# Even mixer of a hybrid decoder step: convolution taps in two chains, sample taps on GpSimd, transposes and layer norm inside the last projection

## The chip, the cores and the metric

One core of one Trainium2 chip runs the whole program: one inference step of a two-layer decoder trunk. The metric is the device time of one execution in microseconds (us). TensorE (PE), VectorE (DVE), ScalarE (ACT) and GpSimd (POOL) each run their own instruction list in order and wait for one another on counting semaphores. SyncE (SP) issues most DMAs.

## The reference, cut to what matters

512 prompt tokens and 64 sample tokens (8 sequences of 8) share all weights. The change concerns the token mixer of layer 0, the "even mixer":

```
def even_mixer(hn, state, W, j):
    a_val, a_gate, q, k, v, o, gates = jnp.split(hn @ W['ev_w_in'][j], SPLIT_EVEN, axis=-1)
    u = a_val * jax.nn.sigmoid(a_gate)
    full = jnp.concatenate([conv_buf, u], axis=1)
    c = lax.conv_general_dilated(full, taps, ...)          # depthwise, 31 taps, 512 channels
    c = c + W['ev_conv_b'][j]
    mu = jnp.mean(c, axis=-1, keepdims=True)
    var = jnp.mean(jnp.square(c - mu), axis=-1, keepdims=True)
    cn = (c - mu) * lax.rsqrt(var + 1e-5) * W['ev_ln_g'][j] + W['ev_ln_b'][j]
    a_out = jax.nn.silu(cn)
    ...
    h, C1, n1, m1 = mlstm_scan(qh, kh, vh, li, lf, C0, n0, m0)
    b_out = jax.nn.sigmoid(o) * h.reshape(B, T, D_B)
    mix = jnp.concatenate([a_out, b_out], axis=-1) @ W['ev_w_out'][j]
```

Around it stand feed-forward blocks, a second mixer and gated embeddings, which the change does not touch.

## The kernel before

Activations lie as features x tokens: 128 partitions by T = 576 columns (SEQ = 512 of the prompt, then 64 of the samples). A projection is a list of weight blocks of 2048 columns, two output tiles to a block. `gemm` multiplies each tile as 8 steps of three products (rounded weight times rounded input, rounded weight times the input's rest, weight's rest times rounded input), each in two pieces of columns. Output tiles alternate between two places in PSUM (`unit`), so tile t starts only when DVE has read tile t-2 (`normed`, semaphore `tile_evacuated`).

A weight block comes by DMA to `raw`, ACT rounds it to `wr` (`round_block`), and GpSimd forms the rest `wl = raw - wr` (line 515). All three work one block ahead of PE.

The even mixer has three projections of four blocks, eight tiles each: `glu` (value and gate of the convolution), `kv`, and `qo` (q, then o). Between `glu` and `kv` PE forms the gate rows of the mLSTM. DVE then computes on four partitions a chain of row operations (lines 1674 to 1707, here "the row chain"), which comes before the first reading of a `kv` tile on DVE.

The convolution runs on DVE. `conv_chunk(slot)` does about eight of the 31 taps of one 128-channel group j: slots 4j to 4j+3. A tap is a multiply-add over 512 prompt columns into PSUM bank 6 (line 1625) and one over the 64 sample columns into bank 7 (line 1628), alternately, so that a multiply-add never waits for the one just ahead of it. The 16 slots stand between readings of projection tiles: slots 0 to 2 in `glu`, 3 to 8 in `kv`, 9 to 15 in `qo`.

After `kv`, PE turns the last two of its tiles, turns the gate rows into columns, and spreads the samples' rows over partitions, each waiting for a copy by ACT. Then comes `qo`. After `qo` come the layer norm of the convolution (sums over channels as products with `ones`, centering, squares, root, scale, SiLU), the spreading of two mLSTM rows for each of four heads (`spread`, line 678), and the first score products. Then the mLSTM runs head by head (`weigh`, `values`, `states`), and last the output projection.

Of the kernel before, what the change touches and what calls it, by code (L numbers as in the profile page):

```python
# [92 lines left out]
def schedule():  # L93
# [32 lines left out]
def build(nc, A):  # L126
# [91 lines left out]
    wgl = sb("wgl", [P, KD, 36], F32R, at=z)  # L218
    kwm = sb("kwm", [SMP, NB, P], at=z)
    smp = sb("smp", [P, HEADS, 3, SMP], at=z)  # L220
# [285 lines left out]
    def _(e):  # L506
        for s in range(2):
            e.nop().then_inc(S(f"w_split{s}"), 1)
        for name in order:
            p = ph[name]  # L510
            with e.Fori(0, p.nb // 2) as i:  # L511
                for s in range(2):

                    e.wait_ge(S("w_rounded"), i * 2 + (p.n0 + s + 1))
                    e.tensor_tensor(wl[s][:, 0:p.width], raw[s][:, 0:p.width],  # L515
                                    wr[s][:, 0:p.width].bitcast(F32), ALU.subtract
                                    ).then_inc(S(f"w_split{s}"), 1)
# [3 lines left out]
    def _(e):  # L521
# [131 lines left out]
        turn_kv(6)  # L653
        turn_kv(7)

        e.wait_ge(S("rows_exp"), 3)
        e.wait_ge(S("turned_copied"), 16)
        for q, row in enumerate((rowa, rowws)):
            for i in range(ST):
                w = P if i < ST - 1 else SMP  # L660
                o = (q * ST + i) * HEADS
                mm = e.transpose(ps[0:w, 4, o:o + HEADS], row[:, i * P:i * P + w],
                                 C("ident", 0, 4, rows=4))
        mm.then_inc(S("cols_turned"), 1)

        e.wait_ge(S("cols_copied"), 4)
        sel = lambda hh: C("sel", hh * P, (hh + 1) * P, rows=4)
        for hh in range(HEADS):
            o = hh % 2 * 3 * SMP
            mm = e.matmul(ps[:, 4 + hh // 2, o:o + 3 * SMP], sel(hh), rows3[:, :, SEQ:T], start=True, stop=True)  # L670
        mm.then_inc(S("smp_ready"), 1)
        gemm("qo", xin, no_wait)
# [7 lines left out]


        e.wait_ge(S("smp_copied"), 2)
        for j in range(TM):
            if j == TM - 1:
                e.wait_ge(S("tile_evacuated"), evac_at("qo", 7))
                spread(0)
                spread(1)
            e.wait_ge(S("conv_done"), j + 1)
            for hf in range(2):
                mm = e.matmul(ps[:, 4 + hf, 0:HALF], ones[:], cv[:, j, hf * HALF:(hf + 1) * HALF],  # L690
                              start=j == 0, stop=j == TM - 1)
        mm.then_inc(S("ln_sum"), 1)
        spread(2)
        spread(3)

# [55 lines left out]

        e.wait_ge(S("ln_centered"), TM)
        scores(0)
        scores(1)

        for j in range(TM):
            e.wait_ge(S("ln_sq"), j + 1)
            for hf in range(2):  # L760
                mm = e.matmul(ps[:, 6 + hf, 0:HALF], ones[:], (hd, sq)[j % 2][:, hf * HALF:(hf + 1) * HALF],
                              start=j == 0, stop=j == TM - 1)
            mm.then_inc(S("ln_var"), 1)
# [266 lines left out]
    def _(e):  # L1030
# [169 lines left out]
        copy_kv(6)  # L1200
        copy_kv(7)
        e.wait_ge(S("cols_turned"), 1)
        for q in range(2):
            o = q * ST * HEADS
            e.activation(gcol[:, o:o + 16], ps[:, 4, o:o + 16], ACT.Copy).then_inc(S("cols_copied"), 1)
            e.activation(gcol[0:SMP, o + 16:o + 20], ps[0:SMP, 4, o + 16:o + 20], ACT.Copy
                         ).then_inc(S("cols_copied"), 1)
        e.wait_ge(S("smp_ready"), 1)
        for q in range(2):
            e.activation(smp[:, 2 * q:2 * q + 2], ps[:, 4 + q, 0:6 * SMP].rearrange("p (h q t) -> p h q t", h=2, q=3),  # L1210
                         ACT.Copy).then_inc(S("smp_copied"), 1)
        for n in blocks("qo"):
            if n >= 2:
                for o in (2 * (n - 2), 2 * (n - 2) + 1):
                    e.wait_ge(S("tile_evacuated"), evac_at("qo", 4 + o))
                    e.activation(oT[:, o, :], tu[:], ACT.Sigmoid).then_inc(S("o_ready"), 1)
# [16 lines left out]
        copy_spread(0)  # L1233
        copy_spread(1)

        e.wait_ge(S("conv_stored"), 16 * (1 + TM))
        for j in range(TM):
            e.wait_ge(S("ln_centered"), j + 1)
            if j >= 2:
                e.wait_ge(S("ln_var"), j - 1)  # L1240
            e.activation((hd, sq)[j % 2][:], cv[:, j, :], ACT.Square).then_inc(S("ln_sq"), 1)
            if j % 2:
                decay(j // 2)

        e.wait_ge(S("ln_var"), TM)
        e.activation(two(acc[:]), ps[:, 6:8, 0:HALF], ACT.Ln, scale=1.0 / DA, bias=eps5[:, 0:1]
                     ).then_inc(S("ln_root"), 1)
        e.wait_ge(S("ln_root"), 1)
        e.activation(acc[:], acc[:], ACT.Exp, scale=-0.5).then_inc(S("ln_root"), 1)
        copy_spread(2)  # L1250
        copy_spread(3)
        for j in range(TM):
            e.wait_ge(S("ln_scaled"), j + 1)
            e.activation(cv[:, j, :], cv[:, j, :], ACT.Silu, scale=W("ln_g", j), bias=W("ln_b", j)
                         ).then_inc(S("conv_out"), 1)
            e.wait_ge(S("conv_out"), j + 1)
            e.activation(xr[:, j, :], cv[:, j, :], ACT.Copy).then_inc(S("mixr_ready"), 1)

# [214 lines left out]
    def _(e):  # L1473
# [137 lines left out]
        accp, accs = ps[:, 6, 0:SEQ], ps[:, 7, 0:SMP].rearrange("p (b t) -> p b t", b=NB)  # L1611

        def tap(j, k, outp, outs, sem=None, wait=None):
# [4 lines left out]
            inp = up[:, j, bass.ds(k, SEQ)]  # L1618
            ins_ = us[:, j, :, bass.ds(k, TB)]
            if wait is None:  # L1620
                a = e.tensor_scalar(outp, inp, w, W("conv_b", j), ALU.mult, ALU.add)
                a.then_inc(S("conv_step"), 1)
                b = e.tensor_scalar(outs, ins_, w, W("conv_b", j), ALU.mult, ALU.add)
            else:
                a = e.scalar_tensor_tensor(outp, inp, w, accp, ALU.mult, ALU.add)
                a.then_inc(S("conv_step"), 1)
# [664 lines left out]
```

## Time and profile before

| what | us |
|---|---|
| median of 3 timed runs | 2624.3 (2612.31 to 2625.74) |
| the profiled execution | 2605.91 |
| its span, first to last instruction | 2604.1 |

The granted clock of TensorE was 0.979 of full speed on average. The profiled execution was shorter than each of the timed runs; durations below are all from it. A wait row names who waited and who ended the wait, and a row of a timeline gives the start, the duration, and in brackets the idle time of the engine just before.

### The profile page before, as it was taken

How to read it: one execution, taken by the hardware profiler on the slowest of the kernel's cores; microseconds unless marked ns; L12 is line 12 of the kernel's file. 1: busy time of each engine (PE TensorE's matmuls, PEld its weight loads, DVE VectorE, ACT ScalarE, POOL GpSimd, SP SyncE). 2: the span in 40 equal slices, each digit the busy share in tenths (PEclk: the TensorE clock that was granted, in tenths of full speed). 3: DMA queues.
4: the chain of work that ended last, by engine and by line, in shares of the span. 5: the costliest groups of instructions: out<-in, count | busy, mean ns of one | idle time of the engine just before them, and what ended most of it. 6: DMA issues, size and time to landing. Idle time of an engine off the chain costs nothing.

```text
span 2604.1 us, 44896 instructions
## 1 busy us (share of the span) xinstructions
PE 2501.4 (96%) x18512; PEld 2401.8 (92%) x18512; DVE 852.9 (33%) x1438; ACT 760.3 (29%) x904; POOL 809.2 (31%) x204
## 2 busy tenths in 40 slices
PE   7999999998779999999999999999989999999997
PEld 7999999987469999999999999999955799999997
DVE  3220222678563220223422112221176532202224
ACT  4221224222323221223432222231155532212232
POOL 3334334322003333333333333343200133343332
PEclk9999999998789999999999999999999999999999
DMA  4222223411112222212222222133442122222222
GB/s 149 81 82 90 81 68 108 93 66 49 34 52 90 81 69 92 91 68 81 83 97 89 73 98 85 63 104 118 145 135 82 49 91 81 77 90 78 70 81 77
DMA packets 67047, 220.67 MB, mean 85 GB/s; under 512 B 14022, under 2 KB 31302, under 8 KB 51338
## 3 DMA queue, kind: packets, MB, share of 16 engines
q1 hardware_dynamic: 56112, 202.84, 23.3%
q10 hardware_dynamic: 10842, 16.53, 2.3%
q8 instruction: 66, 1.08, 0.2%
q14 instruction: 27, 0.22, 0.0%
HBM read 208.02 MB, written 11.33 MB: 84 GB/s over the span
## 4 chain that ended last, share of the span: by engine, by line
issue 55%; PE 31%; POOL 11%; DVE 2%; ACT 0%; POOLq 0%; DMA 0%; DVEq 0%
PE ps L556 26%; POOL wl L515 11%; PE ps L939 2%; DVE rows L1962 0%; PE ps L913 0%; PE ps L825 0%; PE ps L969 0%; PE ps L817 0%; DVE tiny L1965 0%; POOLq L511 0%; PE ps L959 0%; PE ps L587 0%; DVE h L2133 0%; DVE stick L2045 0%; PE ps L991 0%
## 5 line engine op out<-in xcount | busy, mean ns | idle before, releaser
L515 POOL TENSOR_TENSOR wl<-raw,wr 128x2048 fp32r<-128x2048 f32 (+2 forms) x200 | 809.0, 4045 | 1769.6 <-ACT wr L1048 1769.6
L556 PE MATMUL ps<-xr,wr 128*128 128x256 f32 (+1 forms) x2304 | 500.0, 299 | 24.1 <-POOL wl L515 20.0
L556 PE MATMUL ps<-xl,wr 128*128 128x256 f32 (+1 forms) x2304 | 496.6, 297 | 0.0
L556 PE MATMUL ps<-xr,wl 128*128 128x256 f32 (+1 forms) x2304 | 496.0, 297 | 0.0
L1048 ACT ACTIVATE wr<-raw 128x2048 fp32r<-128x2048 f32 (+1 forms) x200 | 351.6, 1758 | 372.0 <-PE ps L556 298.8
L556 PEld LDWEIGHTS ps<-xr,wr 128*128 128x128 f32 x2304 | 390.5, 191 | 27.1 <-issue 19.9
L556 PEld LDWEIGHTS ps<-xl,wr 128*128 128x128 f32 x2304 | 391.1, 191 | 0.0
L556 PEld LDWEIGHTS ps<-xr,wl 128*128 128x128 f32 x2304 | 390.6, 191 | 0.0
L556 PE MATMUL ps<-x2r,wr 128*128 128x256 f32 (+1 forms) x1664 | 354.5, 294 | 0.9 <-POOL wl L515 0.9
L556 PE MATMUL ps<-x2l,wr 128*128 128x256 f32 (+1 forms) x1664 | 353.6, 293 | 0.0
L556 PE MATMUL ps<-x2r,wl 128*128 128x256 f32 (+1 forms) x1664 | 353.5, 293 | 0.0
L556 PE MATMUL ps<-hr,wr 128*128 128x256 f32 x1472 | 313.0, 294 | 0.0
L556 PE MATMUL ps<-hl,wr 128*128 128x256 f32 x1472 | 312.9, 293 | 0.0
L556 PE MATMUL ps<-hr,wl 128*128 128x256 f32 x1472 | 312.8, 293 | 0.0
L556 PEld LDWEIGHTS ps<-x2r,wr 128*128 128x128 f32 x1664 | 277.3, 187 | 1.9 <-issue 1.5
L556 PEld LDWEIGHTS ps<-x2r,wl 128*128 128x128 f32 x1664 | 277.3, 187 | 0.0
L556 PEld LDWEIGHTS ps<-x2l,wr 128*128 128x128 f32 x1664 | 277.1, 187 | 0.0
L556 PEld LDWEIGHTS ps<-hr,wr 128*128 128x128 f32 x1472 | 245.1, 187 | 1.3 <-DVE tu L1521 0.9
L556 PEld LDWEIGHTS ps<-hl,wr 128*128 128x128 f32 x1472 | 245.2, 188 | 0.0
L556 PEld LDWEIGHTS ps<-hr,wl 128*128 128x128 f32 x1472 | 245.2, 187 | 0.0
L1521 DVE TENSOR_TENSOR tu<-ps,R 128x576 f32<-128x576 f32 x96 | 72.7, 758 | 499.9 <-PE ps L556 499.9
L1102 ACT ACTIVATE hr<-hd 128x576 f32 (+1 forms) x88 | 60.5, 687 | 577.9 <-DVE hd L1537 577.9
(305 smaller groups left out, 1852.4 us busy)
## 6 DMA issues: line engine op xcount, KB each, us to landing
raw<-in_up SPq DMA_DIRECT2D x88, 1024.0 KB, 4.9
raw<-in_down SPq DMA_DIRECT2D x32, 768.0 KB, 4.2
raw<-in_mixin SPq DMA_DIRECT2D x24, 1024.0 KB, 4.9
raw<-in_down SPq DMA_DIRECT2D x32, 640.0 KB, 3.9
raw<-in_ple SPq DMA_DIRECT2D x16, 640.0 KB, 3.9
raw<-in_mixout SPq DMA_DIRECT2D x8, 1024.0 KB, 4.9
kc<-in_kc SPq DMA_DIRECT2D x32, 256.0 KB, 3.5
vc<-in_vc SPq DMA_DIRECT2D x32, 256.0 KB, 3.0
```

Source lines behind the costliest of these rows:

```text
L515: e.tensor_tensor(wl[s][:, 0:p.width], raw[s][:, 0:p.width], wr[s][:, 0:p.width].bitcast(F32), ALU.subtract).then_inc(S(f"w_split{s}"), 1)
L556: mm = e.matmul(piece(u, hf), w_[:, a:b], x_[:, x0:x1], start=n_k == 0 and n_ == 0, stop=n_k == kn_ - 1 and n_ == 2)
L939: mm = e.matmul(ps[:, 2 + c, o:w], C("after" if j == i else "later"), stick[hh % 2][:, c, at:at + w - o], start=j == i, stop=j == TM - 1)
L1048: e.activation(wr[slot][:, 0:w], raw[slot][:, 0:w], ACT.Copy).then_inc(S("w_rounded"), 1)
L1102: e.activation(column(hr, i * 2 + s), hd[:], ACT.Copy).then_inc(S("hr_ready"), 1)
L1521: ins = e.tensor_tensor(out, unit(u), R[:], ALU.mult)
```

## The change

- The last projection is renamed `oq` and makes o's four tiles first, then q's; the host's order of weight tiles follows.
- The prompt's taps go in two chains: even steps add up in PSUM bank 6, odd ones in bank 7. A tap waits for the tap before the last. A final addition joins the two.
- The samples' taps go to GpSimd (`conv_of_samples`): for half of a channel group, one product over 32 positions x 31 taps, four halving additions, one last addition and the bias, each waiting for the one before. Eight such halves stand behind the splits of blocks `glu` 2 to `oq` 1.
- The slots move forward: 0 to 6 in `glu`, 7 to 13 in `kv`, 14 and 15 in `oq`.
- PE's work between `kv` and the last projection, and the two products of the layer norm, stand between tiles of `oq`. ACT's copies, squares, root and SiLU, and DVE's centering and scaling, move with them.
- The rounding of the convolution's output (`xr`), the input of the output projection, stays behind `oq`.

```
+        def conv_of_samples(n):
+            j, half = divmod(n, 2)
+            e.wait_ge(S("u_ready"), 2 * j + 2)
...
+            e.tensor_tensor(prods[:].rearrange("p (b t) k -> p b t k", t=TB), windows,
+                            taps.unsqueeze(1).unsqueeze(1).broadcast_to([P, NB // 2, TB, TAPS]), ALU.mult
+                            ).then_inc(S("sample_added"), 1)
+            for a, b in ((15, 16), (8, 8), (4, 4), (2, 2)):
+                e.wait_ge(S("sample_added"), added[0])
+                e.tensor_tensor(prods[:, :, 0:a], prods[:, :, 0:a], prods[:, :, b:b + a], ALU.add
+                                ).then_inc(S("sample_added"), 1)
...
+        SAMPLES_BEHIND = {("glu", 2): 0, ("glu", 3): 1, ("kv", 0): 2, ("kv", 1): 3, ("kv", 2): 4, ("kv", 3): 5,
+                          ("oq", 0): 6, ("oq", 1): 7}
...
-        turn_kv(6)
-        turn_kv(7)
...
+        beside_oq = {0: lambda: turn_kv(6), 1: lambda: turn_kv(7), 2: turn_gates, 3: spread_samples, 5: ln_sums,
+                     6: ln_squares}
+        gemm("oq", xin, no_wait, lambda t: beside_oq[t]() if t in beside_oq else None)
...
+        e.wait_ge(S("tile_evacuated"), evac_at("oq", 7))
         e.wait_ge(S("ln_centered"), TM)
+        spread(0)
         scores(0)
+        spread(1)
         scores(1)
+        spread(2)
+        spread(3)
...
-            if wait is not None:
-                e.wait_ge(S("conv_step"), wait - 1)
...
-                b = e.scalar_tensor_tensor(outs, ins_, w, accs, ALU.mult, ALU.add)
+            e.wait_ge(S("conv_step"), n - 1)
+            e.scalar_tensor_tensor(chain[q], up[:, j, bass.ds(k, SEQ)], w, chain[q], ALU.mult, ALU.add
+                                   ).then_inc(S("conv_step"), 1)
...
-            if j < TM - 1:
-                conv_chunk(j)
+            for slot in ((0,), (1, 2), (3, 4), (5, 6))[j]:
+                conv_chunk(slot)
...
-            if t >= 2:
-                conv_chunk(t + 1)
+            if t:
+                conv_chunk(6 + t)
...
+            if t < 2:
+                conv_chunk(14 + t)
+            if t == 5:
+                e.wait_ge(S("ln_sum"), 1)
+                for j in range(TM):
+                    e.scalar_tensor_tensor(two(cv[:, j, :]), psn, -1.0 / DA, two(cv[:, j, :]), ALU.mult, ALU.add
+                                           ).then_inc(S("ln_centered"), 1)
+            if t == 6:
+                e.wait_ge(S("ln_root"), 2)
+                for j in range(TM):
+                    e.tensor_tensor(cv[:, j, :], cv[:, j, :], acc[:], ALU.mult).then_inc(S("ln_scaled"), 1)
```

The order of instructions at three places follows. First DVE at the end of `glu`: the readings of tiles 6 and 7 (`tg`, `tu`), the convolution's input `up` and `us`, and the start of the row chain (`rowa`). Before:

```order
L1521 TENSOR_TENSOR tg<-ps,R 128x576 [waits tile_done]
L1521 TENSOR_TENSOR tu<-ps,R 128x576 [waits tile_done]
L1660 TENSOR_TENSOR up<-tg,sg 128x512 [waits tile_evacuated,glu_sig]
L1661 TENSOR_TENSOR us<-tg,sg 128x8x8
L1674 TENSOR_TENSOR rowa<-ps,R 4x576 [waits gates_done,u_ready]
L1675 TENSOR_TENSOR rowt<-ps,R 4x576
```

After the change (one of the two loops of taps, slot 6, shown; each loop body has two taps):

```order
L1702 UNCONDITIONAL_BRANCH
L1702 ISA
L1685 ISA [waits conv_step]
L1685 SCALAR_TENSOR_TENSOR ps<-up,prm,ps 128x512
L1684 REGISTER_ALU
L1685 ISA [waits conv_step]
L1685 SCALAR_TENSOR_TENSOR ps<-up,prm,ps 128x512
L1702 REGISTER_ALU
L1702 COMPARE_AND_BRANCH
L1734 TENSOR_TENSOR rowa<-ps,R 4x576 [waits gates_done]
L1735 TENSOR_TENSOR rowt<-ps,R 4x576
```

The row chain stood right behind `us`; now sixteen taps stand between them, and the sample instruction (L1628) is gone from the loop.

Second, GpSimd behind the split of a block in the changed kernel, where before one split followed the other:

```order
L515 TENSOR_TENSOR wl_55<-raw_52,wr_54 128x2048 [waits w_rounded]
L531 TENSOR_TENSOR prods<-us,prm 128x992 [waits sample_conv,u_ready]
L537 TENSOR_TENSOR prods<-prods 128x32x15 [waits sample_added]
L537 TENSOR_TENSOR prods<-prods 128x32x8 [waits sample_added]
L537 TENSOR_TENSOR prods<-prods 128x32x4 [waits sample_added]
L537 TENSOR_TENSOR prods<-prods 128x32x2 [waits sample_added]
L542 TENSOR_TENSOR cv<-prods 128x32 [waits sample_added]
L545 TENSOR_SCALAR cv<-cv,prm 128x32 [waits sample_added]
L515 TENSOR_TENSOR wl_57<-raw_53,wr_56 128x2048 [waits w_rounded]
```

Seven short instructions came between two splits.

Third, PE behind the last tile of the last projection. Before (the sums of the layer norm's last group, spreading, scores, the first of the squares):

```order
L690 MATMUL ps<-cv,ones 128x288 [waits conv_done]
L690 MATMUL ps<-cv,ones 128x288
L678 MATMUL ps<-rows_100,cst 128x512 [waits bcast_copied]
L678 MATMUL ps<-rows_100,cst 128x512
L678 MATMUL ps<-rows_100,cst 128x512 [waits bcast_copied]
L678 MATMUL ps<-rows_100,cst 128x512
L707 MATMUL ps<-qT,kT 128x512 [waits ln_centered]
L707 MATMUL ps<-qT,kT 128x384
L761 MATMUL ps<-hd,ones 128x288 [waits ln_sq]
```

After:

```order
L746 MATMUL ps<-rows_100,cst 128x512 [waits ln_centered,tile_evacuated]
L746 MATMUL ps<-rows_100,cst 128x512
L757 MATMUL ps<-qT,kT 128x512
L746 MATMUL ps<-rows_100,cst 128x512 x2
L757 MATMUL ps<-qT,kT 128x384
L746 MATMUL ps<-rows_100,cst 128x512 [waits bcast_copied]
L746 MATMUL ps<-rows_100,cst 128x512
L746 MATMUL ps<-rows_100,cst 128x512 [waits bcast_copied]
L746 MATMUL ps<-rows_100,cst 128x512
L770 MATMUL ps<-tg,vn 128x512 [waits p_ready,vn_ones,bcast_copied]
```

The products with `ones` have left this place, and the first value product (L770) follows the spreading directly.

## Rows read from the trace of the kernel before

**Rows 1.** The page: busy time of each engine over the span.

```profile
PE 2501.4 (96%) x18512; PEld 2401.8 (92%) x18512; DVE 852.9 (33%) x1438; ACT 760.3 (29%) x904; POOL 809.2 (31%) x204
```

**Rows 2.** Busy time by stretch; PEclk is the granted clock of TensorE.

```profile
core 0: us, PE busy (x) PEld busy (x) DVE busy (x) ACT busy (x) POOL busy (x), PEclk, DMA share, GB/s
505.00:561.10 56.10, 54.58 (x415) 54.34 (x414) 46.97 (x92) 15.82 (x21) 18.77 (x4) 1.00 0.46 81
561.10:572.20 11.10, 5.67 (x31) 4.45 (x28) 10.91 (x24) 2.62 (x10) 0.00 (x0) 0.77 0.01 2
572.20:577.30 5.10, 5.10 (x22) 5.09 (x22) 1.46 (x4) 2.67 (x3) 2.24 (x1) 0.50 0.00 2
577.30:637.80 60.50, 52.10 (x378) 50.65 (x376) 55.43 (x116) 9.02 (x8) 16.30 (x4) 0.98 0.20 70
637.80:654.20 16.40, 16.40 (x20) 6.12 (x20) 3.48 (x6) 5.99 (x9) 0.00 (x0) 0.50 0.00 0
654.20:674.10 19.90, 13.90 (x33) 7.58 (x32) 7.94 (x14) 12.96 (x19) 0.00 (x0) 0.79 0.03 4
```

**Rows 3.** Timeline of DVE in `glu`: tile readings, taps.

```profile
473.23 0.76 DVE L1521 TENSOR_TENSOR tu<-ps,R 128x576 f32<-128x576 f32 x1 [1.32 <-PE ps L556]
...
476.01 0.76 DVE L1625 SCALAR_TENSOR_TENSOR ps<-up,prm,ps 128x512 f32<-128x512 f32 x1 [0.44 <-DVE us L1661]
476.67 0.28 DVE L1628 SCALAR_TENSOR_TENSOR ps<-us,prm,ps 128x64 f32<-128x64 f32 x1
476.94 0.76 DVE L1625 SCALAR_TENSOR_TENSOR ps<-up,prm,ps 128x512 f32<-128x512 f32 x1
...
483.63 0.75 DVE L1521 TENSOR_TENSOR tg<-ps,R 128x576 f32<-128x576 f32 x1
486.03 0.76 DVE L1521 TENSOR_TENSOR tu<-ps,R 128x576 f32<-128x576 f32 x1 [1.64 <-PE ps L556]
```

**Rows 4.** Timeline of DVE: the row chain and the first readings of `kv`.

```profile
505.22 0.75 DVE L1674 TENSOR_TENSOR rowa<-ps,R 4x576 f32<-4x576 f32 x1 [4.06 <-PE ps L527]
...
510.67 2.15 DVE L1689 SCALAR_TENSOR_TENSOR rowt<-rowt,rowB 4x576 f32<-4x576 f32 x1 [1.59 <-ACT rowB L1188]
...
518.28 0.20 DVE L1707 TENSOR_TENSOR rowws<-rowa,rows 4x64 f32<-4x64 f32 x1
518.51 1.42 DVE L1523 SCALAR_TENSOR_TENSOR kT<-ps,R 128x576 f32<-128x576 f32 x2
```

**Rows 5.** Timeline of POOL: the split beside that row chain.

```profile
507.29 4.92 POOL L515 TENSOR_TENSOR wl<-raw,wr 128x2048 fp32r<-128x2048 f32 x1 [13.28 <-ACT wr L1048]
```

**Rows 6.** Groups of DVE, 300 to 900 us: an addition's kind with two SBUF inputs.

```profile
L1537 DVE TENSOR_TENSOR hd<-tu,sg 128x576 f32<-128x576 f32 x13 | 9.8, 758 | 0.5
```

**Rows 7.** Groups of POOL by shape, whole span: busy us, mean ns.

```profile
L515 POOL TENSOR_TENSOR wl<-raw,wr 128x2048 fp32r<-128x2048 f32 x120 | 554.9, 4624 | 1294.4 <-ACT wr L1048 1294.4
L515 POOL TENSOR_TENSOR wl<-raw,wr 128x1280 fp32r<-128x1280 f32 x48 | 141.8, 2955 | 272.2 <-ACT wr L1048 272.2
```

**Rows 8.** Timeline of PE: turning, sample rows, spreading, scores, sums of squares.

```profile
560.62 0.71 PE L645 MATMUL ps<-cst,sq 128*128 128x128 f32 x5
...
569.35 2.92 PE L670 MATMUL ps<-rows,cst 4*128 4x192 f32 x8 [0.45 <-ACT gcol L1206]
...
637.76 7.19 PE L678 MATMUL ps<-rows,cst 4*128 4x512 f32 x8 [5.90 <-DVE tu L1521]
...
654.22 3.35 PE L707 MATMUL ps<-qT,kT 128*128 128x512 f32 x4
...
659.27 1.13 PE L761 MATMUL ps<-sq,ones 128*128 128x288 f32 x4
```

**Rows 9.** Timeline of ACT, then of DVE: rounding of the convolution's output, and the next gap of `weigh`.

```profile
671.08 0.68 ACT L1257 ACTIVATE xr<-cv 128x576 fp32r<-128x576 f32 x1
...
674.06 0.29 DVE L1734 TENSOR_SCALAR Xs<-Mb,gcol 128x128 f32<-128x128 f32 x1
```

More of the change, by code:

```diff
@@ L509, in _ @@
+        SAMPLES_BEHIND = {("glu", 2): 0, ("glu", 3): 1, ("kv", 0): 2, ("kv", 1): 3, ("kv", 2): 4, ("kv", 3): 5,
+                          ("oq", 0): 6, ("oq", 1): 7}
         for name in order:
             p = ph[name]
+            if name in ("glu", "kv", "oq"):
+                for n in range(p.nb):
+                    split(p, n // 2, n % 2)
+                    if (name, n) in SAMPLES_BEHIND:
+                        conv_of_samples(SAMPLES_BEHIND[name, n])
+                continue
             with e.Fori(0, p.nb // 2) as i:
@@ L664, in _, with turn_gates @@
-        mm.then_inc(S("cols_turned"), 1)
-        e.wait_ge(S("cols_copied"), 4)
-        sel = lambda hh: C("sel", hh * P, (hh + 1) * P, rows=4)
[L668 to L672, printed above, removed]
+        def turn_gates():
+            e.wait_ge(S("rows_exp"), 3)
+            e.wait_ge(S("turned_copied"), 16)
+            for q, row in enumerate((rowa, rowws)):
+                for i in range(ST):
+                    w = P if i < ST - 1 else SMP
+                    o = (q * ST + i) * HEADS
+                    mm = e.transpose(ps[0:w, 4, o:o + HEADS], row[:, i * P:i * P + w],
+                                     C("ident", 0, 4, rows=4))
+            mm.then_inc(S("cols_turned"), 1)
@@ new lines, in ln_squares @@
+        def ln_squares():
+            for j in range(TM):
+                e.wait_ge(S("ln_sq"), j + 1)
+                for hf in range(2):
+                    mm = e.matmul(ps[:, 6 + hf, 0:HALF], ones[:], (hd, sq)[j % 2][:, hf * HALF:(hf + 1) * HALF],
+                                  start=j == 0, stop=j == TM - 1)
+                mm.then_inc(S("ln_var"), 1)
+        beside_oq = {0: lambda: turn_kv(6), 1: lambda: turn_kv(7), 2: turn_gates, 3: spread_samples, 5: ln_sums,
+                     6: ln_squares}
@@ L679, in spread @@
             mm.then_inc(S("bcast_ready"), 1)
[L682 to L694, printed above, removed]
         def scores(k):
@@ L1212, in _, with copy_gates @@
[L1212 to L1216, printed above, removed]
+        def copy_gates():
+            e.wait_ge(S("cols_turned"), 1)
+            for q in range(2):
+                o = q * ST * HEADS
+                e.activation(gcol[:, o:o + 16], ps[:, 4, o:o + 16], ACT.Copy).then_inc(S("cols_copied"), 1)
+                e.activation(gcol[0:SMP, o + 16:o + 20], ps[0:SMP, 4, o + 16:o + 20], ACT.Copy
+                             ).then_inc(S("cols_copied"), 1)
@@ L1233, in _ @@
         copy_spread(0)
+        decay(0)
         copy_spread(1)
-        e.wait_ge(S("conv_stored"), 16 * (1 + TM))
+        decay(1)
+        for hh in (2, 3):
+            copy_spread(hh)
         for j in range(TM):
[L1238 to L1255, printed above, removed]
+            e.wait_ge(S("tile_done"), done_at("oq", 7))
             e.wait_ge(S("conv_out"), j + 1)
             e.activation(xr[:, j, :], cv[:, j, :], ACT.Copy).then_inc(S("mixr_ready"), 1)
+        e.wait_ge(S("conv_stored"), 16 * (1 + TM))
+        e.wait_ge(S("conv_done"), TM)
+        e.wait_ge(S("sample_conv"), 2 * TM)
         def load_state(hh):
@@ L1752, in weigh @@
             e.tensor_tensor(pm[0:r, 0:n], pm[0:r, 0:n], m, ALU.mult).then_inc(S("p_ready"), 1)
-        e.wait_ge(S("ln_sum"), 1)
-        for j in range(TM):
-            e.scalar_tensor_tensor(two(cv[:, j, :]), psn, -1.0 / DA, two(cv[:, j, :]), ALU.mult, ALU.add
-                                   ).then_inc(S("ln_centered"), 1)
         e.wait_ge(S("bcast_copied"), 2)
@@ L1764, in _ @@
         weigh(1)
-        e.wait_ge(S("ln_root"), 2)
-        for j in range(TM):
-            e.tensor_tensor(cv[:, j, :], cv[:, j, :], acc[:], ALU.mult).then_inc(S("ln_scaled"), 1)
         for j in range(TM):
```

158 lines of the change are left out of this document (97 added, 61 removed).

## The prediction

> **What bounds the kernel now.** I read the page first: PE is busy for 96% of the span, DVE for a third [rows 1]. So outside the even mixer another engine's work is free, and a gain must come from stretches in which PE stands idle or runs cold. The table by stretch shows four such places. Over `kv` (505.0 to 561.1 us) PE is nearly full at full clock. In the 11.1 us behind it PE is half busy, with turning and spreading that wait for ACT's copies. The 5.1 us after that run at a granted clock of 0.50. The last projection then takes until 637.8, though DVE is busy for 55.4 of its last 60.5 us: DVE sets the pace there, not PE. From 637.8 to 674.1 PE does layer norm and spreading, at first at clock 0.50 [rows 2].
>
> The timeline of DVE gives the prices. Two tiles of a projection are 12.8 us apart on PE (473.23 and 486.03, the readings of the odd tiles, each just after its tile ends), so a tile is 6.4 us. A prompt tap has 0.66 us from its start to the next instruction's, though it lasts 0.76; a pair of prompt and sample takes 0.93 to 1.0 [rows 3]. Eight pairs (about 7.7 us) and a reading are longer than 6.4, which is why DVE leads in the last projection.
>
> **The change part by part.** The sum compares times on the profiled execution, up to the start of `weigh`'s fourth gap, at 674.06 [rows 9]; what follows is the same in both.
>
> *Taps in `glu`.* Without the sample instruction a tap should cost 0.66, the pair's 0.97 less some 0.3. This trace has no two taps in a row; the bounds are 0.66 and 0.76, a tap's whole duration, if the next must wait for its end. I take 0.66, since it is the row's distance to an instruction that depends on the tap before the last, as now. But the slots move forward. Behind group 1's input come two slots instead of one: 476.01 + 16 x 0.66 + 0.2 for two loop entries = 486.8, then the reading of tile 4, to 487.5. PE wanted its place at 485.8: it waits 1.7. Tile 5 is read at once; from such a reading to the next first tap there are 2.78 us (473.23 to 476.01), so slots 3 and 4 start at 490.2. They hold 12 taps (7.9), two opening products (1.4), the last tap and its dependent addition (1.5) and entries (0.2): until 501.3. Two readings and again 2.78 lead to 504.7; slots 5 and 6 last 10.8, until 515.5.
>
> *The row chain* stood right behind; it began at 505.22 and the first reading of `kv` at 518.51 [rows 4], 13.3 us. It now begins at 515.5 and ends at 528.8. This is the wait that the change adds: behind the chain on DVE stands the reading of `kv` tiles 0 and 1, and PE's tile 2 waits for that. PE has done tiles 0 and 1 at about 519.6 and then has nothing: its third tile starts some 10.3 us later than before.
>
> *The chain beside GpSimd.* In the chain one multiply-add of 4x576 with two SBUF inputs took 2.15 us [rows 4] where a larger two-input operation takes 0.76 [rows 6]; a split on GpSimd ran from 507.29 to 512.21 [rows 5], and the slow one ended 0.6 after that. So a two-input instruction stood still until GpSimd's ended. The tap, with one input in PSUM, keeps 0.76 beside a split. Now GpSimd works through most of the chain's time, first a half of samples, then a split. Five long operations of the chain have two SBUF inputs. Between none of them hit (-1.4) and one behind a whole split (4.6), one behind a product (2.3) and some behind short additions (1), I take +2, little over what was seen once. PE's tile 2 of `kv`: 10.3 + 2 = **+12.3**.
>
> The Trainium skill (SBUF — State Buffer, § SBUF: two separate sides) says that DVE's two-input operations and GpSimd share a port pair as an exclusive lock, held for the whole instruction by whoever starts first. By that rule the delay is the upper end, about +8, and the forecast falls by 6; the slow row of the chain agrees with it, but how often the two meet depends on instants.
>
> *The clock after that wait.* Behind the idle stretch at 561 to 572 the clock was 0.50 for 5.1 us of the next projection [rows 2]: half of that, 2.5 us, was lost. An idle time of some 12 us in `kv` should cost the same: **+2.5** (bounds 0 and 5). From there `kv` runs at PE's pace: a tile and a turning are under 7 us, a reading and a slot 0.7 + 5.5.
>
> *Behind `kv`.* Its 11.1 us go: **-11.1**.
>
> *The last projection.* Before: 572.2 to 637.8, 65.6 us. After: eight tiles, 51.2; two turnings at 0.5 (five products took 0.71 to the end of the last), the gate columns 1, the sample rows 1.5 (2.92 at half clock), two rounds of four sums at 1.13 each, 9.0 [rows 8]; then the reading of the last tile, 0.9. With 1 us for the hand-overs of the squares and 0.5 for DVE's scaling, a two-input operation beside the split of the next block, this makes 66.1: **+0.5**. DVE no longer leads: two slots are left here, and centering and scaling (four operations each of 0.67) fit beside a tile.
>
> *Behind it.* Before: 637.8 to 674.06, 36.3 us. What is left: the spreading of four heads, twice the row of 7.19, and the scores, 3.35, all at clock 0.50 [rows 2, 8], so 17.7, or 8.9 at full clock; the copy of the last pair, 1.2, four roundings, 0.6 from start to start (0.68 each, [rows 9]), and the last subtraction, 0.8. That is 13.2 at full clock and 22.0 at half. PE comes warm from the projection; but 16.4 us of such work at 100% busy did not lift the clock before [rows 2], so it may fall on the way. I take full clock for all but some 2 us: 15.3, so **-21** (bounds -14.3 and -23.1).
>
> *Samples on GpSimd.* Two shapes give 2.17 ns a column and 0.175 us for an instruction [rows 7]. A half has 992 + 480 + 256 + 128 + 64 + 32 + 32 = 1984 columns in seven instructions: 4.3 + 1.2 + waits of some 0.5, about 6.0 us. With its split, 4.6, that is 10.6 of a block's 12.8. The next split is wanted 12.8 us after this one, and PE wants its result 6 us after that. So I put it at nothing; its cover ends at 8.2 us a half, and much of what it overruns is hidden by the wait in `kv`.
>
> Sum: 12.3 + 2.5 - 11.1 + 0.5 - 21 = -16.8, say **-17**: a span of 2587 where it was 2604.1. The execution lasted 2605.91, that is 18.4 below the median of the timed runs, 2624.3; I apply the difference to the median: **2607 us**. A change under 0.5%, 13 us, can't be told from none; the runs before lie 13 us apart.
>
> **The rivals.**
>
> *The port decides (0.12).* The chain's two-input operations wait +8 instead of +2, and the scaling another 2. The row of 2.15 speaks for it; against it, DVE also takes turns, and five operations can't all fall on long ones. 17 - 8 = 9 gained: 2615, no change.
>
> *Spreading runs cold (0.08).* -14.3 instead of -21: 10 gained, 2614. For it: the clock row of 637.8 to 654.2; against: that stretch began after 6 us without PE work.
>
> *The chains buy little (0.07).* If a tap takes 0.97 as the pair did, 44 taps up to the row chain add 0.31 x 44 = 13.6 to the wait in `kv`, and a slot of 7.8 with its reading paces `kv` again: 2621 to 2626, no change. At 0.76 it is 0.1 x 44 = 4.4, and 2611.
>
> *GpSimd is the bound (0.12), slower.* From its first split with a half, 463.8, GpSimd has eight splits and halves and then the split for the third block of the last projection, which PE wants at about 605. With c for a half, that split ends at 463.8 + 8 x (4.6 + c) + 4.6. The gain of 17 is gone when this is 622, at c = 14.6, 2.4 times my estimate or 1.2 us more per instruction. At 18 us it ends at 649: 44 late, a loss of 27, 2651. For it: no row shows a short, strided or broadcast instruction there, or a scalar operation; against: 0.175 us is all that the two shapes leave for the start of one.
>
> **How the numbers follow.** The forecast's own case, a gain of 13 to 24 (2600 to 2611), has 0.54; a gain beyond that, with none of the port's waits and everything warm, 0.07. Faster is 0.61. Same: 0.12 + 0.08 + 0.07 = 0.27. Slower: 0.12. With the bounds of the terms (port -1.4 to +8, clock 0 to 5, spreading -14.3 to -23.1) the gain runs from 2 to 25; with the timed runs' spread of 13 around the median the range is 2589 to 2627, which leaves out most of the slower case and the extremes.
>
> **What the changed profile would show.** Right: taps of one group 0.66 apart; PE idle in `kv` before tile 2 for 10 to 14 us, ended by DVE's reading, with clock 0.50 behind it; no idle stretch between `kv` and the last projection; that projection in about 65 us with 9 us of products with `ones` in it; the fourth gap of `weigh` near 657. It would be wrong if PE waits for splits (line 515), if halves of samples last over 8 us, or if that idle in `kv` is much under 8 or over 18 us.

## The result, and the profile after

Timed, the changed kernel takes 2603.2 us (median of 7 runs, 2596.4 to 2608.0), the kernel before 2613.6 (7 runs, 2609.3 to 2625.7): a ratio of 0.9931, with a 95% interval of 0.9911 to 0.995. The profiled execution took 2601.26 us for a span of 2599.5; before, the span was 2604.1. The medians differ by 10 us, the ratio says 18, the two spans 4.6. The runs of the kernel before lie in two groups, at 2609 to 2614 and at 2624 to 2626 us, so its median and each ratio to it depend on how many runs fall in the upper one; with the longer times the record shows a lower mean granted clock (2609 us at 0.977, 2626 at 0.971, in runs timed beside the experiments), and no trace of a longer run was taken. And behind the changed part, where the programs are the same, the two profiled executions are 4 us apart (1930.0 us from the fourth gap to the end before, 1934.0 after). So the parts of the change are read at points inside it, up to the fourth gap of `weigh`, as the prediction did.

The same points after, first the page's busy time, to be held against [rows 1], then the busy time by stretch, against [rows 2] (PEclk is the granted clock of TensorE):

```profile
PE 2497.4 (96%) x18512; PEld 2401.3 (92%) x18512; DVE 834.3 (32%) x1318; ACT 759.7 (29%) x904; POOL 856.0 (33%) x260
```

```profile
core 0: us, PE busy (x) PEld busy (x) DVE busy (x) ACT busy (x) POOL busy (x), PEclk, DMA share, GB/s
519.00:535.40 16.40, 0.15 (x2) 0.04 (x1) 15.28 (x15) 4.52 (x6) 13.79 (x12) 0.58 0.30 108
535.40:538.60 3.20, 3.20 (x13) 3.20 (x14) 3.20 (x6) 0.00 (x0) 0.00 (x0) 0.50 0.00 0
538.60:578.50 39.90, 39.90 (x306) 39.90 (x305) 33.04 (x50) 7.37 (x12) 20.43 (x16) 1.00 0.15 54
578.50:643.60 65.10, 63.02 (x448) 60.23 (x445) 31.05 (x41) 23.66 (x33) 24.02 (x11) 1.00 0.18 59
643.60:644.50 0.90, 0.82 (x2) 0.48 (x3) 0.03 (x1) 0.88 (x2) 0.00 (x0) 1.00 0.93 391
644.50:664.90 20.40, 19.23 (x23) 6.19 (x22) 5.12 (x11) 8.90 (x16) 0.00 (x0) 0.50 0.13 42
```

The reader is to see three things. PE now stands idle for 16.2 us in `kv`, ahead of its tile 2, and for the 3.2 us behind that it runs at clock 0.50. From 538.6 to 643.6 there is no idle stretch between `kv` and the last projection, which takes 65.1 us. And from 644.5 on, with PE busy nearly all the time, the clock is 0.50 for 20.4 us.

What PE waited for, from `glu` to the start of the spreading (us in total, times, longest):

```profile
PE ps L598 <- DVE kT L1591: 16.2, 1, 16.2
PE ps L746 <- DVE qT L1589: 2.2, 1, 2.2
PE ps L598 <- DVE tg L1589: 1.4, 1, 1.4
```

The row chain on DVE, which stands before that reading of `kT`; it answers to [rows 4] (start, duration, operation):

```profile
514.14 0.74 DVE L1734 TENSOR_TENSOR rowa<-ps,R 4x576 f32<-4x576 f32 x1
...
515.69 1.10 DVE L1737 TENSOR_SCALAR rowa<-rowa,prm 4x576 f32<-4x576 f32 x1
516.72 1.48 DVE L1738 TENSOR_SCALAR rowt<-rowt,prm 4x576 f32<-4x576 f32 x1
...
522.54 4.87 DVE L1753 TENSOR_TENSOR rowa<-rowa,rowB 4x576 f32<-4x576 f32 x1
527.44 2.29 DVE L1756 COPY rowt<-rowa 4x576 f32<-4x576 f32 x1
529.76 1.07 DVE L1759 TENSOR_TENSOR rowt<-rowa,prm 4x8 f32<-4x8 f32 x1
...
534.49 1.42 DVE L1591 SCALAR_TENSOR_TENSOR kT<-ps,R 128x576 f32<-128x576 f32 x2
```

And GpSimd (POOL) beside it: a split, a half of samples (product, additions), the next split, the next half:

```profile
514.27 2.21 POOL L531 TENSOR_TENSOR prods<-us,prm 128x992 f32<-128x992 f32 x1
516.55 3.24 POOL L537 TENSOR_TENSOR prods<-prods 128x480 f32<-128x480 f32 x4
...
522.23 4.57 POOL L515 TENSOR_TENSOR wl<-raw,wr 128x2048 fp32r<-128x2048 f32 x1 [1.64 <-ACT wr L1096]
526.76 2.66 POOL L531 TENSOR_TENSOR prods<-us,prm 128x992 f32<-128x992 f32 x1
529.50 4.88 POOL L537 TENSOR_TENSOR prods<-prods 128x480 f32<-128x480 f32 x4
```

The chain lasts 20.3 us where it took 13.3. Put the two lists side by side: the subtraction of 4.87 us starts 0.3 us behind the start of the split at 522.23 and ends 0.6 behind its end; the copy of 2.29 us starts within the product of 526.76 and ends 0.3 behind its end; an operation on 4x8 numbers takes 1.07 us.

Behind the last projection (PE, then DVE; it answers to [rows 8, 9]):

```profile
643.68 2.87 PE L746 MATMUL ps<-rows,cst 4*128 4x512 f32 x4 [2.17 <-DVE qT L1589]
646.48 2.08 PE L757 MATMUL ps<-qT,kT 128*128 128x512 f32 x2
648.48 3.78 PE L746 MATMUL ps<-rows,cst 4*128 4x512 f32 x4
...
653.77 7.19 PE L746 MATMUL ps<-rows,cst 4*128 4x512 f32 x8
```

```profile
665.49 0.29 DVE L1804 TENSOR_SCALAR Xs<-Mb,gcol 128x128 f32<-128x128 f32 x1
```

The fourth gap of `weigh` stands at 665.49, where it was at 674.06: 8.6 us earlier. The last eight of the 16 spreading products take as long as before, 7.19 us.

### The profile page after: what moved, and what is told of

Read it like the earlier page. It is cut to its first block, busy times and chain, and to the rows that moved or that the text cites. A ratio compares the mean times of both kernels' runs of the same rounds, so it can differ in the third digit from the quotient of the medians.

```text
span 2599.5 us, 44514 instructions
## 1 busy us (share of the span) xinstructions
PE 2497.4 (96%) x18512; PEld 2401.3 (92%) x18512; DVE 834.3 (32%) x1318; ACT 759.7 (29%) x904; POOL 856.0 (33%) x260
## 4 chain that ended last, share of the span: by engine, by line
PE 50%; issue 37%; POOL 7%; DVE 3%; ACT 1%; DVEq 0%; POOLq 0%; DMA 0%
PE ps L598 46%; POOL wl L515 7%; PE ps L987 2%; DVE ps L1685 0%; DVE rows L2024 0%; PE ps L873 0%; PE ps L961 0%; PE ps L1017 0%; PE ps L629 0%; PE ps L687 0%; PE ps L865 0%; DVE tiny L2027 0%; PE ps L1007 0%; DVE h L2195 0%; PE ps L645 0%
```

## The experiments

Nine kernels were timed, in three sets on three chips, each set with the kernel before beside it; that had medians of 2622.9 (the late slots, the halves, the taps, the full height), 2613.7 (the split, the 32 rows, the five products, the four edits) and 2616.3 (the order). The ratios are those to the kernel before in the same set. Two numbers compare the kernels with the changed kernel: the place of the fourth gap in the trace, and the median.

| kernel | median | ratio to the kernel before (95% interval) | fourth gap | against the changed kernel: gap, median |
|---|---|---|---|---|
| before | 2613.6 | 1 | 674.06 | +8.6, +10.4 |
| changed | 2603.2 | 0.9931 (0.9911 to 0.995) | 665.49 | |
| late slots | 2589.2 | 0.9884 (0.9858 to 0.9909) | 652.92 | -12.6, -14.0 |
| halves off the chain | 2598.0 | 0.9911 (0.989 to 0.9931) | 663.50 | -2.0, -5.2 |
| taps only | 2611.5 | 0.9953 (0.9934 to 0.9972) | 672.07 | +6.6, +8.3 |
| order only | 2615.6 | 0.9991 (0.9977 to 1.0005) | 680.51 | +15.0, +12.4 |
| split after scaling | 2603.4 | 0.9961 (0.9948 to 0.9974) | 663.57 | -1.9, +0.1 |
| full height | 2594.9 | 0.9895 (0.9873 to 0.9916) | 659.12 | -6.4, -8.3 |
| 32 rows | 2602.2 | 0.9954 (0.9932 to 0.9975) | 666.43 | +0.9, -1.0 |
| five products | 2628.6 | 1.0061 (1.004 to 1.0082) | 690.68 | +25.2, +25.4 |
| four edits | 2577.2 | 0.9866 (0.9848 to 0.9884) | 640.71 | -24.8, -26.0 |

The last column's two numbers agree within 3.2 us for every kernel, across the sets. The ratios of different sets agree less well, because the kernel before moves under them. A gap also carries what the execution was early or late ahead of the changed work: at the reading of `glu`'s second tile (460.06 us in the changed kernel) the halves stand 1.6 us later, the order 1.4, the four edits 1.3 and the others up to 0.7. Without that the halves gain 3.6 on the changed kernel and the four edits 26.0, the order loses 13.6, and the change itself gained 8.2.

**The slots later.** The row chain starts later because slots were put ahead of it.

```
-            for slot in ((0,), (1, 2), (3, 4), (5, 6))[j]:
+            for slot in ((0,), (1,), (2,), ())[j]:
...
-            if t:
-                conv_chunk(6 + t)
+            conv_chunk(3 + t)
...
-            if t < 2:
-                conv_chunk(14 + t)
+            if t < 5:
+                conv_chunk(11 + t)
```

> Edit: behind the gated inputs of glu stand slots 0, 1 and 2 alone, one for each of the first three groups; 3 to 10 follow the eight readings of kv, 11 to 15 the first five of the last projection. My account (the idle time of 16.25 us in kv is the row chain's late start, 514.1, and the rest of its 20.3 us is the port): the chain starts at 503 to 504, lasts between 13.3 and 20.3 us and ends at 517 to 524; PE wants the place of kv's tile 2 at about 519, so that wait falls to 0 to 5 us, the stretch at granted clock 0.50 behind it goes, and the kernel gains 12 to 17 on the changed one: 2586 to 2592. Rival 1: the five slots that now lie in the last projection make DVE its pace-maker again (before, DVE was busy for 55.4 of 60.5 us there): that projection takes 70 us or more instead of 65, and the kernel gains under 8: 2595 or more. Rival 2: the length of the chain is what GpSimd makes of it wherever it stands, and it meets a split and two halves here too, lasting 25 us or more: 2595 or more, with a wait of 10 us left in kv.

2589.2 us; the fourth gap comes 12.6 earlier. The wait for `kT` is 5.0 us, and the last projection has no new wait. My account held, but for two points: the chain started at 505.10, not at 503 to 504, and the cold stretch behind the wait did not go, the clock was 0.50 from 522.7 to 525.8. The chain ended at 521.87: its rows on DVE show that GpSimd beside it still costs 3.5 us, and that a scan, which has two inputs in SBUF too, is held up as well (it takes 1.35 alone):

```profile
510.68 2.04 DVE L1749 SCALAR_TENSOR_TENSOR rowt<-rowt,rowB 4x576 f32<-4x576 f32 x1 [1.72 <-ACT rowB L1236]
512.76 3.25 DVE L1751 TENSOR_TENSOR_SCAN rowB<-rows,rowt 4x576 f32<-4x576 f32 x1
516.04 1.61 DVE L1753 TENSOR_TENSOR rowa<-rowa,rowB 4x576 f32<-4x576 f32 x1
```

**The halves away from the chain.**

```
-        SAMPLES_BEHIND = {("glu", 2): 0, ("glu", 3): 1, ("kv", 0): 2, ("kv", 1): 3, ("kv", 2): 4, ("kv", 3): 5,
-                          ("oq", 0): 6, ("oq", 1): 7}
+        SAMPLES_BEHIND = {("glu", 2): (0,), ("glu", 3): (1,), ("kv", 0): (2, 3), ("kv", 3): (4,),
+                          ("oq", 0): (5,), ("oq", 1): (6,), ("oq", 2): (7,)}
...
```

> Edit: the two halves of samples that GpSimd works on while the row chain runs (514 to 521 and 527 to 535) are put elsewhere, one behind kv's first split beside the half that is there, the others a block later each; the splits stay. My account (DVE's operations of the chain stood behind GpSimd's instructions): the scalar additions (1.10 and 1.48 us) go back to some 0.5, the copy (2.29) to 0.45, the maximum (1.07) to 0.16, the last addition (1.15) to 0.75; only the subtraction (4.87) behind the split stays. The chain lasts 15 instead of 20.3 us, the wait for kT falls from 16.25 to about 11, and the kernel comes to about 2598. Rival: what slows the chain is the splits, or operations that wait for each other, and not the halves: the chain stays within 2 us of 20.3 and the time at 2603.

2598.0 us. The chain's rows (DVE), the same operations as in the list above:

```profile
517.43 0.74 DVE L1734 TENSOR_TENSOR rowa<-ps,R 4x576 f32<-4x576 f32 x1
...
518.98 0.51 DVE L1737 TENSOR_SCALAR rowa<-rowa,prm 4x576 f32<-4x576 f32 x1
519.42 0.50 DVE L1738 TENSOR_SCALAR rowt<-rowt,prm 4x576 f32<-4x576 f32 x1
...
524.26 4.87 DVE L1753 TENSOR_TENSOR rowa<-rowa,rowB 4x576 f32<-4x576 f32 x1
529.16 0.45 DVE L1756 COPY rowt<-rowa 4x576 f32<-4x576 f32 x1
529.64 0.16 DVE L1759 TENSOR_TENSOR rowt<-rowa,prm 4x8 f32<-4x8 f32 x1
...
532.66 1.42 DVE L1591 SCALAR_TENSOR_TENSOR kT<-ps,R 128x576 f32<-128x576 f32 x2
```

Each went to the duration expected of it, and the subtraction behind the split alone stayed. The chain takes 15.2 us, so GpSimd's instructions are shown to be what slows it. The time gained less than the 5 us of the chain: the half that was moved forward met DVE's two-input multiplications of `glu` instead (1.37 and 1.26 us where they take 0.69 and 0.22). That put the start of the chain 1.7 us later; the other 1.6 of its 3.3 (to 517.43) this execution was late already in `glu`. The wait for `kT` fell to 12.9, not 11, and the gain is 2.0 by the fourth gap, 3.6 without the late start, and 5 by the medians, where I expected 5.

**One half of the change at a time.** First the taps in two chains and the samples on GpSimd, everything else, the slots too, as before:

> Edit: the kernel before, with q before o, the turning and the layer norm behind the projection and its slots at their old places, but with the taps in two chains and the samples' taps on GpSimd. My account (before, DVE led in the last projection, 65.6 us where PE needs 51.2 and a reading): the projection takes 52 to 54 us, the row chain loses 0 to 7 us beside GpSimd, the cold stretches stay. A gain of 6 to 13 on the kernel before, so by its median of 2613.6 of the runs here 2600 to 2607: as much as the whole change gave. Rival: what the change gave came from the new order on PE, and the cheaper taps alone move work off an engine that ended no wait: within 4 us of the kernel before.

2611.5 us, 0.9953: 11 us under the kernel before in its set, as expected, but that stood at 2622.9 there. By its own median, where I expected 2600 to 2607, and by the fourth gap, 2.0 earlier than before, it is hardly faster. The projection does what I expected: its tiles, read up to 8.3 us apart before, come every 6.40 (592.04, 598.44, 604.84, 611.24). But the row chain takes 24.4 us beside the halves, 11 more than before and well over my 0 to 7, and gives that back. Here an operation with one input in SBUF stood behind a whole split, and one on 4x64 numbers too:

```profile
507.43 4.88 DVE L1713 TENSOR_SCALAR rowt<-rowt,prm 4x576 f32<-4x576 f32 x1
...
521.85 4.50 DVE L1739 TENSOR_TENSOR rows<-prm,rows 4x64 f32<-4x64 f32 x1
```

Then the other half, the new order on PE and ACT with o before q and the slots as in the changed kernel, but with the old taps:

> Edit: the other half of the undoing. The new order on PE and ACT, o before q and the slots at the changed kernel's places stay; the taps are the old ones again, pairs of a prompt's and a sample's instruction on DVE, and GpSimd has its splits alone. My account (the new order needs the cheap taps): the pairs of 0.97 instead of 0.66 us put the row chain some 10 to 14 us later, to 524 to 528; without halves beside it, it lasts 13 to 18 us; so kv's tile 2 waits 22 to 28 us instead of 16, and a slot with its reading, 8.5 us, paces the tiles of kv behind it (7 tiles, 1.6 us each over PE's 6.95): 2613 to 2627, no gain on the kernel before or a loss. Rival: the order on PE is what gave the gain, and DVE's longer slots hide beside PE's turning and layer norm: within 5 us of the changed kernel, 2599 to 2608.

2615.6 us, 0.9991: no gain, and by the fourth gap 6.5 later than before. The chain started at 529.61, and PE waited 18.4 us for `kT` (I expected 22 to 28) and 6.3 instead of 1.4 for a tile of `glu`. DVE read the tiles of `kv` behind that mostly 8.28 us apart, but PE still turned one every 6.95 (574.44, 581.39, 588.34) and paid only at the end of `kv`, with 2.6 and 1.1 us of waiting for ACT's copies of the last tiles. Without halves on GpSimd the chain takes 15.2 us. So neither half is worth much alone: at the fourth gap the taps bring 2.0, the order costs 6.5, and both together bring 8.6. With the old taps the new order starts the row chain 15 us later still, and with the halves of samples beside it the chain of the old order is 11 us longer.

**The split behind the scaling.** In the changed kernel the first scaling on DVE takes 3.93 us beside GpSimd's split for the output projection.

```
+            if name == ("out", 0):
+                e.wait_ge(S("ln_scaled"), TM)
```

> Edit: GpSimd's split for the first block of the output projection waits until DVE has scaled all four groups. My account: DVE's first scaling (3.93 us in the changed kernel, beside that split) takes 0.75, so the reading of the last tile comes about 2.2 to 3.2 us earlier and PE's wait of 2.2 us ahead of the spreading goes. On the clock that leaves two theories. A: the clock falls behind the idle time of 2.5 us ahead of the spreading; without it the spreading starts and stays at 1.00, and the kernel gains 8 to 12: 2591 to 2595. B: the products with four rows do not hold the clock; it falls all the same some microseconds into them, and the gain is the 2 us alone: 2600 to 2602.

2603.4 us. The four scalings take 2.77 us instead of 5.94 together, PE's wait ahead of the spreading is 0.8 instead of 2.2, the fourth gap comes 1.9 earlier, and the clock falls all the same, 2.1 us into the spreading (theory B). The medians show nothing of the 1.9 (theory B gave 2600 to 2602). The clock:

```profile
642.70:644.90 2.20, 2.09 (x5) 0.84 (x6) 0.06 (x1) 0.57 (x2) 2.20 (x1) 1.00 0.00 0
644.90:663.50 18.60, 17.42 (x20) 5.83 (x21) 5.65 (x11) 7.90 (x15) 0.10 (x1) 0.50 0.33 109
```

**The spreading at full height.** The products that spread rows over the partitions take four rows of the array.

```
-    rows3 = sb("rows3", [HEADS, 3, T], at=z)
+    rows_all = sb("rows_all", [P, 3, T], at=z)
+    rows3 = rows_all[0:HEADS]
...
-            for q, row in enumerate((rowM, rowem)):
-                mm = e.matmul(ps[:, 2 * (hh % 2) + q, :], sel(hh), row[:, 0:SEQ], start=True, stop=True)
+            for q in range(2):
+                mm = e.matmul(ps[:, 2 * (hh % 2) + q, :], C("sel", hh * P, (hh + 1) * P), rows_all[:, q, 0:SEQ],
+                              start=True, stop=True)
...
+        step(e.memset(rows_all[:, 0:2, 0:SEQ], 0.0))
+        settle()
```

> Edit: the rows that are spread over the partitions stand in a block of 128 rows of which 124 are zero, and the products that spread them take all 128 rows instead of four; two memsets ahead of glu (1024 columns each 128 rows) are added; the result is the same. Theory 1 (TensorE ran at granted clock 0.50 from 644.4 to 664.9 because it did products with four rows there): the spreading and the scores run at 1.00, spread products of 0.9 instead of 1.8 us each, and the fourth gap comes 7 to 9 us earlier: 2594 to 2597. Theory 2 (the clock falls for another reason, the wait of 2.2 us ahead of it or the waits for copies within it): the clock stays at 0.50 there and the time within 3 us of 2603.

2594.9 us. The clock by stretch, from the spreading to the fourth gap:

```profile
644.20:645.70 1.50, 1.44 (x3) 0.68 (x4) 0.00 (x1) 1.48 (x2) 0.00 (x0) 0.96 0.61 257
645.70:649.00 3.30, 3.30 (x5) 1.35 (x4) 0.82 (x2) 1.95 (x4) 0.00 (x0) 0.50 0.00 0
649.00:659.10 10.10, 8.92 (x24) 4.21 (x23) 4.86 (x9) 6.33 (x13) 0.00 (x0) 1.00 0.30 103
```

The clock falls here too, but comes back after 3.3 us, and eight spreading products take 3.60 us instead of 7.19:

```profile
651.00 3.60 PE L747 MATMUL ps<-rows_all,cst 128*128 128x512 f32 x8
```

The fourth gap is at 659.12, 14.9 us behind the start of the spreading, where it was 21.8: 6.4 us earlier, a little under the 7 to 9 expected. Theory 1, then, with a correction: the clock falls with 128 rows too, so here the four rows are not shown to make it fall; they keep it down. The same with a block of 32 rows:

> Edit: as the spreading with 128 rows, but the block has 32 rows (28 of them zero). The 128 rows brought the clock back to 1.00 after 3.4 us where four rows left it at 0.50 for 20.5. If what brings it back is how much of the array's height a product fills, 32 rows lie between: I expect that they do not do it, a cold stretch of over 15 us and 2600 to 2605. If anything above four rows does it: a cold stretch of some 3.4 us and 2593 to 2597.

2602.2 us. The clock stayed down, as with four:

```profile
644.20:644.90 0.70, 0.63 (x2) 0.39 (x3) 0.01 (x1) 0.68 (x2) 0.00 (x0) 0.98 1.06 445
644.90:666.40 21.50, 20.32 (x24) 6.67 (x23) 5.67 (x11) 9.09 (x16) 0.00 (x0) 0.50 0.14 50
```

PE was busy for 20.32 of those 21.50 us. Keeping PE busy was not enough, then.

**GpSimd loaded.** To see how near the slower rival was, each half makes its products five times.

```
+            for again in range(5):
+                if again:
+                    e.wait_ge(S("sample_added"), added[0])
...
```

> Edit: in each half GpSimd makes the products of the samples five times in a row instead of once, with the same result. A half then takes 6.1 + 4 x 2.25 = 15.1 us, just over the 14.6 from which the prediction let GpSimd eat the whole gain. By the working of that rival the split for the third block of the last projection ends at 463.4 + 8 x (4.6 + 15.1) + 4.6 = 625.6, and PE wants it at about 607: waits of 18 us in all for splits, and 0 to 5 us more of the row chain beside more products. 2620 to 2626. Against it: GpSimd is idle for long stretches in kv, and the late splits hide in the idle time of 16 us there; then under 8 us are lost, 2603 to 2611.

2628.6 us, slower than the kernel before (1.0061). The first half took 15.4 us. PE's waits:

```profile
PE ps L601 <- DVE kT L1594: 23.3, 1, 23.3
PE ps L601 <- POOL wl L515: 7.2, 2, 4.9
PE ps L601 <- DVE tg L1592: 3.5, 1, 3.5
```

The size was nearly right (2620 to 2626 expected), the way only in part. Waits for splits are 7.2 us and not 18; as much, 7.1, was lost at `kT` and 2.1 more at `tg`, because DVE's gated inputs in `glu` and the row chain stood behind the products; the rest of the 25 us is not split up here. The first of these inputs:

```profile
491.10 2.41 DVE L1724 TENSOR_TENSOR up<-tg,sg 128x512 f32<-128x512 f32 x1 [0.75 <-ACT sg L1212]
```

**The edits together.** The late slots, the split behind the scaling, the spreading at full height, and no half behind the split that runs beside the chain.

> Edit: the late slots, the spreading with 128 rows and the split behind the scaling together, and of the samples' halves none behind the split that runs beside the row chain (the others follow one block later). My account adds the terms: the row chain lasts 13.3 to 14 us from 505, so of the wait of 16.25 us in kv 0 to 1.5 are left and the cold 1.6 behind it go (-16 to -18), the wait of 2.2 ahead of the spreading goes (-2), and the spreading is cold for at most 3.4 us (-6 to -8). Together -24 to -28 on the changed kernel: 2575 to 2579, 0.983 to 0.985 of the kernel before. Rival: the edits get in each other's way, the last half of samples, which now stands behind the third split of the last projection, or the slot in its fifth tile holds up the layer norm's sums: 2585 or more, with a wait for GpSimd or DVE in that projection.

2577.2 us, the fastest of all, 26 under the changed kernel and 0.9866 of the kernel before (I expected 0.983 to 0.985). The clock and PE's waits:

```profile
627.40:640.70 13.30, 11.97 (x30) 5.65 (x31) 5.77 (x12) 8.51 (x16) 2.35 (x1) 1.00 0.44 151
```

```profile
PE ps L601 <- DVE kT L1595: 1.8, 1, 1.8
PE ps L749 <- DVE qT L1593: 0.8, 1, 0.8
```

The row chain takes 13.6 us, the wait for `kT` is 1.8, and the spreading up to the fourth gap (640.71) runs at 1.00 throughout, in 13.3 us. The terms add up as expected, 24.8 us at the fourth gap, but for one: behind the wait of only 1.8 us in `kv` the clock still averaged 0.53 from 521.2 to 524.6, where I had counted that cold stretch as gone.

## Why the prediction came out as it did

The forecast was 2607, a gain of 17 on 2624.3; measured was 2603.2, a gain of 10 on 2613.6, and 8.6 at the fourth gap. The time fits by luck, because two errors met: the median of three runs that I subtracted from, 2624.3, lies 10.7 us above the median of seven; and the gain is half of what I had. Term by term, each between the same two points of both traces:

| from, to | forecast | measured |
|---|---|---|
| start of the row chain | +10.3 | +8.9 (505.22 to 514.14) |
| length of the row chain | +2 | +7.0 (13.3 to 20.3) |
| from the first reading of `kv` to the spreading: clock, tail, last projection | +2.5 - 11.1 + 0.5 = -8.1 | -10.1 (119.3 to 109.2) |
| from the spreading to the fourth gap | -21 | -14.5 (36.3 to 21.8) |
| sum, rounding aside | -17 | -8.6 |

*Taps and slots: right.* Four taps in a row took 2.73 us at 0.75 each, so 0.66 apart; the place in `glu` was waited for 1.4 us (forecast 1.7). The half of samples takes 6.1 us where DVE leaves it alone (forecast 6.0), and no split was waited for. But the half beside the end of the row chain took 8.4 (526.76 to 535.17), over the 8 that I had named as a sign of being wrong: DVE held GpSimd up in turn, which I had not thought of, and the next split, at 553.74, hid it.

*The chain beside GpSimd: the mechanism right, the size not.* I took +2 between -1.4 and +8; it is +7, near the +8 of the rival "the port decides" (0.12). Of the 7, the subtraction behind the whole split is 4.1, a case that stood in my bounds and got little weight; the two scalar additions and the copy are 3.4, which stood nowhere; shorter two-input operations are 1.7; and the multiply-add and a wait for ACT gave back 2.2. So the step that failed is that I counted "five long operations of the chain" with two SBUF inputs, and little on those. The traces show one-input operations between SBUF and SBUF held up as well: the scalar additions, the copy, and, with the taps alone, 4.88 us for one behind a whole split. Away from the halves they take 0.45 to 0.51 for 576 columns, where a two-input operation takes 0.75. The Trainium skill (VectorE: DVE Perf Modes, § Mode 2×_2P) says that such an operation reads one tensor through both ports, which these durations agree with, and (SBUF — State Buffer, § SBUF: two separate sides) that this mode asks for the shared pair too. The section was in front of me, and I used only half of its rule. Taps, with an input in PSUM, were not held up, as forecast.

*The wait in `kv`: right in kind, too small.* 16.2 us, where I gave 10 to 14; the excess comes from the length of the chain, which started 1.4 earlier than forecast. The clock behind it cost less than forecast: 3.2 us at 0.50, some 1.6.

*From `kv` to the spreading: 2 better than forecast.* Half of it is the clock in `kv`, 1.5 us from PE's first product of tile 2 to its sixth turning (42.7 us where it was 41.2) instead of 2.5. The other half is the last projection: 65.1 us is 1.0 under the forecast in spite of 2.2 us of waiting for the scaling, the first of which took 3.93 beside a split, 3.2 more than alone, where I had 0.5. The 11.1 us behind `kv` went as forecast, though not only for the reason that I gave, "turning and spreading that wait for ACT's copies": in the kernel before, DVE read the last tiles of `kv` 8.3 us apart while PE turned one every 6.95, and the longest wait there was for DVE's late reading of `sg` (rows of DVE, then of PE):

```profile
549.83 0.75 DVE L1521 TENSOR_TENSOR sq<-ps,R 128x576 f32<-128x576 f32 x1
558.12 0.75 DVE L1521 TENSOR_TENSOR tg<-ps,R 128x576 f32<-128x576 f32 x1
...
546.73 0.71 PE L645 MATMUL ps<-cst,kT 128*128 128x128 f32 x5
...
553.68 0.71 PE L645 MATMUL ps<-cst,hd 128*128 128x128 f32 x5
...
566.11 0.77 PE L645 MATMUL ps<-cst,sg 128*128 128x128 f32 x5 [3.11 <-DVE sg L1521]
```

*Behind the projection: the step that failed.* "PE comes warm from the projection", and I took full clock for all but 2 us. It came warm, and 0.8 us into the spreading the clock was 0.50, for 20.4 us. What I had put in the rival, 0.08, is what happened: -14.5, between its -14.3 and my -21. My evidence against it, that the cold stretch before "began after 6 us without PE work", did not decide: with only 0.8 us of waiting left the clock fell as well, with 128 rows behind 2.2 us of waiting it recovered, and in the four edits together, with 128 rows behind 0.8 us, it did not fall there at all. At full clock the stretch takes 13.3 us, which is what I had worked out for it (13.2). The Trainium skill (TensorE: Matmul & The Clock Gate, § Part 1) ties the gate to how busy PE has been; here PE at 94% busy stayed at the lower level when most of its products filled 4 or 32 rows, and the measurement decides.

*The slower rival.* At 15.4 us a half the gain was gone and more, but the larger part of the waits that came with it was for DVE, which stood behind GpSimd (9.2 us), and not for late splits (7.2).

The change as a whole: the cheap taps and the new order need each other, as the two halves show. What they could have brought went into the wait for the row chain (16 us) and into a spreading at half clock (8 us). Of these the late slots gave back 12.6, the full height 6.4 (by the fourth gap).

What stays open: why the clock fell in the spreading with 128 rows when that edit stood alone (3.3 us) and not with the other edits. The wait ahead of the spreading was 2.2 us in the one and 0.8 in the other, and no run separates that from the rest.

## What to carry to other kernels

Work that is taken off a waiting engine must not be put ahead of what the bound engine waits for: ask at each place where slots are filled which instruction stands behind them. Before moving work to GpSimd, list all that DVE does meanwhile between SBUF and SBUF, with one input or two, however small, and count the whole length of GpSimd's instruction for what meets it. And before counting on TensorE's full clock, look at how many rows its products fill, not only at whether it is busy: that was worth 6.4 us here.

## What the hardware showed that was not expected

- TensorE's granted clock stayed at 0.50 (1.2 GHz) for 20.4 us in which most products fill 4 rows (19.2 us of it busy) and for 21.5 us with 32 rows; with 128 rows, 124 of them zero, it was back at 1.00 (2.4 GHz) after 3.3 us.
- The cold stretch did not grow with the wait: behind 16.2 us without PE work in `kv` the clock was 0.50 for 3.2 us, behind 12.9 (halves) for 4.9, behind 5.0 (late slots) for 3.1, and behind 1.8 (four edits) it averaged 0.53 for 3.4.
- DVE's one-input fp32 operations from SBUF to SBUF were held up by a running GpSimd instruction: 4.88 us instead of 0.50 behind a split, 2.29 instead of 0.45 for a copy. Memsets beside GpSimd kept their 0.54 us.
- It goes both ways: GpSimd's four additions took 4.88 us beside the chain, 3.24 beside less of it, 3.06 away from it.
- GpSimd's short instructions cost little: 0.26 us for an addition of 32 columns and 0.36 for a scalar one, where the straight line through two long shapes left 0.24.
